# A hybrid decoder layer on one core: nine buffers for gathered index keys, and work moved at the opening and at the output block

## The reference

```
h = rmsnorm(x);  z = h @ w_in            # 2048 x 8848, columns shared among the parts below
retention (8 heads of 128): rotary on q, k; chunks of 128 tokens
    o = (q k^T * decay) v + (q s) * q_decay;  s' = g^c s + (k * k_decay)^T v
    r = head_group_norm(o) * silu(gate)
sparse attention (8 query heads, 2 kv heads), for each query:
    score = sum_h w_h * relu(q_h . k_idx)  over 16 index heads
    top 128 keys (prompt) or top 256 of 4097 cached and new keys (samples)
    a = softmax(q k_sel^T / sqrt(128)) v_sel * silu(gate)
y = rmsnorm(x + concat(r, a) @ w_out)    # 2048 x 2048
```

## Time and profile before

| | |
|---|---|
| median of 3 runs | 1228.62 us |
| the profiled execution | 1228.03 us |
| its span | 1225.6 us |
| TensorE busy | 1173.5 us (96%) |
| VectorE, ScalarE, GpSimd busy | 628.8, 452.2, 569.7 us |
| mean granted TensorE clock | 0.994 |

### The profile page before, as it was taken

How to read it: one execution, slowest core, us unless ns; L and a number is a source line. 1 busy time by engine, 2 the same in 40 slices (tenths; PEclk the granted TensorE clock), 3 DMA queues, 4 the chain that set the end, 5 groups by cost and what they waited for, 6 DMA issues and landing times.

```text
span 1225.6 us, 21932 instructions
## 1 busy us (share of the span) xinstructions
PE 1173.5 (96%) x9168; PEld 1107.1 (90%) x9168; DVE 628.8 (51%) x1198; ACT 452.2 (37%) x790; POOL 569.7 (46%) x255
## 2 busy tenths in 40 slices
PE   6999999888999999999999989999999999999995
PEld 4999996446999999999999989999999998999995
DVE  6600005997996995799997314343442546010013
ACT  5332225664223333333424323442524252233332
POOL 2346454241433333223635485946666384535450
PEclk9999999999999999999999999999999999999998
DMA  7333435272232222222243416445353425432313
GB/s 243 103 108 107 137 103 205 97 258 94 70 115 93 70 70 84 92 70 69 70 124 98 112 35 175 112 114 159 104 152 91 140 70 189 143 103 74 98 35 139
DMA packets 152840, 138.58 MB, mean 113 GB/s; under 512 B 4653, under 2 KB 145053, under 8 KB 151069
## 3 DMA queue, kind: packets, MB, share of 16 engines
q1 hardware_dynamic: 144502, 110.72, 30.1%
q0 software_dynamic: 6976, 22.03, 5.5%
q10 hardware_dynamic: 1280, 4.66, 1.0%
HBM read 127.02 MB, written 10.34 MB: 112 GB/s over the span
## 4 chain that ended last, share of the span: by engine, by line
PE 81%; DVE 10%; DMA 4%; POOL 2%; issue 2%; ACT 1%; another core or an unknown queue 0%; DVEq 0%; ACTq 0%; POOLq 0%
PE bank L1440 23%; PE bank L1441 23%; PE bank L1442 23%; PE bank L1458 4%; DMA kx<-in_cache_kidx,pidx 3%; DVE bm L1077 2%; PE bank L1645 1%; PE bank L1663 1%; DVE cand L1143 1%; DVE top L1139 1%; DVE besti L1141 1%; DMA XT<-in_x_prompt 1%; PE bank L1685 1%; POOL rowf L889 1%; PE bank L1818 1%
## 5 line engine op out<-in xcount | busy, mean ns | idle before, releaser
L1440 PE MATMUL bank<-Hh,Wh 128*128 128x264 f32 (+2 forms) x2432 | 711.2, 292 | 3.0 <-DVE Hl L1277 0.8
L1441 PE MATMUL bank<-Hl,Wh 128*128 128x264 f32 (+2 forms) x2432 | 702.4, 289 | 0.8 <-issue 0.8
L1442 PE MATMUL bank<-Hh,Wl 128*128 128x264 f32 (+2 forms) x2432 | 701.1, 288 | 0.0
L839 POOL TENSOR_TENSOR Wl<-Wraw,Wh 128x2048 fp32r<-128x2048 f32 x84 | 387.2, 4610 | 476.6 <-ACT Wh L487 475.9
L1440 PEld LDWEIGHTS bank<-Hh,Wh 128*128 128x128 f32 x2432 | 458.7, 189 | 8.6 <-issue 4.2
L1441 PEld LDWEIGHTS bank<-Hl,Wh 128*128 128x128 f32 x2432 | 458.5, 189 | 3.0 <-issue 2.7
L1442 PEld LDWEIGHTS bank<-Hh,Wl 128*128 128x128 f32 x2432 | 457.6, 188 | 0.5 <-issue 0.5
L487 ACT ACTIVATE Wh<-Wraw 128x2048 fp32r<-128x2048 f32 x84 | 160.4, 1911 | 362.9 <-PE bank L1442 362.7
L1380 DVE TENSOR_TENSOR Y<-Y,bank 128x512 f32 (+1 forms) x16 | 10.4, 685 | 159.2 <-PE bank L1458 159.2
L1060 DVE COPY QS<-mix 128x128 f32<-128x128 f32 x1 | 0.3, 275 | 140.5 <-ACT mix L493 140.5
L865 POOL DMA_INDIRECT kx<-in_cache_kidx,pidx x32 | 30.3, 947 | 52.6 <-PE bank L1458 46.1
(11 more groups left out here) (255 smaller groups left out, 1230.6 us busy)
## 6 DMA issues: line engine op xcount, KB each, us to landing
Wraw<-in_w_in SPq DMA_DIRECT2D x36, 1024.0 KB
Wraw<-in_w_in SPq DMA_DIRECT2D x64, 512.0 KB
Wraw<-in_w_out SPq DMA_DIRECT2D x16, 1024.0 KB
XT<-in_x_prompt ACTq DMA_DIRECT2D x4, 1024.0 KB, 9.1
sp__96<-in_state_ret SPq DMA_DIRECT2D x8, 512.0 KB, 4.1
out<-sp__96 SPq DMA_DIRECT2D x8, 512.0 KB, 5.3
Y<-in_x_prompt SPq DMA_DIRECT2D x1, 4096.0 KB
out<-Y SPq DMA_DIRECT2D x4, 1024.0 KB
```

The lines of the kernel that those rows point to most:

```text
L839: nc.gpsimd.tensor_tensor(Wl[:, a, :, :], Wraw[:, a, :, :], Wh[:, a, :, :].bitcast(F32), ALU.subtract).then_inc(w_lo, 1)
L1440: mm(bank[i][:, 0:w], wh, Hh[:, kk, s], start=(a == 0 and k == 0), stop=False)
L1441: mm(bank[i][:, 0:w], wh, Hl[:, kk, s], start=False, stop=False)
L1442: last = mm(bank[i][:, 0:w], wl, Hh[:, kk, s], start=False, stop=(a == 1 and k == KC - 1))
```

## The change

It has five parts.

1. Opening: tiles 2 and 3 are turned earlier (tile 2 right behind the samples, tile 3 ahead of `index_weights`), 24 transposes of the constant stand ahead of the first turn (in bank 6), 8 instead of 24 behind the second, and 4 between the key halves go.
2. Cached keys: nine buffers `kx` instead of six; the six slots of `kT` move into `mix`, where gates are stored later. Buffers 2 to 4 lie where `kT` and the new index keys were, so GpSimd waits for `kin_out` before gather 2 and ScalarE doesn't.
3. Retention head 0: 12 top-k steps instead of 14 ahead of `gate(7)`.
4. Output block: `outputs(7)` moves behind the first part of block 35, `turn_outputs(7)` from ahead of the third part to ahead of the fourth; on VectorE three of four `mix_low(1)` go ahead of the samples' norm, the fourth behind `gated(7)`.
5. Tail: GpSimd multiplies the samples' rows by the gain too; the last scaling of y_sample is shared between VectorE and ScalarE.

```diff
+NKX = 9
-        kT, o3 = place("kT", [P, 6, T], F32, o)
-        QS, o3 = place("QS", [P, NS * 32], F32, o3)
+        kT = mix[:, 0:6, 0:T]
+        QS, o3 = place("QS", [P, NS * 32], F32, o + 3 * 4 * KPR * P)
-        for i in range(6):
-            off = (at["scores"][0], at["best"][0])[i] if i < 2 else o3
+        for i in range(NKX):
+            off = (at["scores"][0], at["best"][0])[i] if i < 2 else o + 4 * KPR * P * (i - 2) if i < 5 else o3
...
+            sp.wait_ge(fin_act, 3)
             store(y_sample.rearrange("b o m -> (b o) m"), Ys[:, :])
...
-            act.wait_ge(kin_out, 32)
             for u in range(4):
                 keys_out(u)
...
             y_scale(2)
+            nc.scalar.activation(Ys[:, LASTC // 2:LASTC], Ys[:, LASTC // 2:LASTC], ACT.Copy,
+                                 scale=st4[0:NS, 44:45]).then_inc(fin_act, 1)
...
             for v in range(4 * 8):
                 s, b = v // NS, v % NS
-                if v >= 6:
-                    w = v - 6
+                if v == 2:
+                    pool.wait_ge(kin_out, 32)
+                if v >= NKX:
+                    w = v - NKX
                     pool.wait_ge(kx_tr, 8 * (w // 4) + 4 + w % 4 + 1)
...
                 nc.gpsimd.tensor_tensor(Y[:, :, c], Y[:, :, c], gfb[:, c].unsqueeze(1).to_broadcast([P, QT, 256]),
-                                        ALU.mult).then_inc(y_gain, 1)
+                                        ALU.mult)
+                nc.gpsimd.tensor_tensor(Ys[:, c], Ys[:, c], gfb[0:NS, c], ALU.mult).then_inc(y_gain, 1)
...
-            def mix_low(half):
+            def mix_low(half, which=range(4)):
-                for i in range(KC * half + 1, KC * half + KC, 2):
+                for i in range(KC * half + 1 + 2 * which.start, KC * half + 1 + 2 * which.stop, 2):
...
                 if h == 0:
-                    topk(14)
+                    topk(12)
                     gate(7)
...
             samples_low(KC, 1)
+            mix_low(1, range(3))
             dve.wait_ge(os_ev, NH)
...
             gated(NH - 1)
+            mix_low(1, range(3, 4))
             dve.wait_ge(gs_tr, 1)
...
-            mix_low(1)
             samples_low(0, 2)
...
-            v_.scalar_tensor_tensor(Ys[:, :], Ys[:, :], st4[0:NS, 44:45], gfb[0:NS, :], ALU.mult, ALU.mult).then_inc(fin_dve, 1)
+            v_.scalar_tensor_tensor(Ys[:, LASTC:DM], Ys[:, LASTC:DM], st4[0:NS, 44:45], gfb[0:NS, LASTC:DM], ALU.mult, ALU.mult)
+            v_.tensor_scalar(Ys[:, 0:LASTC // 2], Ys[:, 0:LASTC // 2], st4[0:NS, 44:45], None, ALU.mult).then_inc(fin_dve, 1)
...
-            def chunk(n, a, between=None, step=None, at_=2):
+            def chunk(n, a, between={}, step=None):
-                    if place_ == at_ and between:
-                        between()
+                    if place_ in between:
+                        between[place_]()
...
-            pe.wait_ge(x_norm, 1)
+            keep_busy(24, 6)
             turn_tokens(0)
             turn_tokens(1)
...
-            keep_busy(24)
+            keep_busy(8, 3)
             pe.wait_ge(h_lo, 8)
             pe.wait_ge(w_lo, 1)
             index_keys(0, slice(0, CUT))
             turn_tokens(2)
-            keep_busy(4)
+            turn_tokens(3)
             pe.wait_ge(w_lo, 2)
             index_keys(1, slice(0, CUT)).then_inc(acc_done, 1)
-            turn_tokens(3)
+            turn_tokens(4)
             index_weights(slice(P, CUT))
-            turn_tokens(4)
...
-            outputs(NH - 1)
-            chunk(NB_IN, 0, lambda: turn_outputs(NH - 1))
+            chunk(NB_IN, 0, {1: lambda: outputs(NH - 1), 3: lambda: turn_outputs(NH - 1)})
```

More of the change, by code:

```diff
@@ L161, in build @@
         kx = []
-        for i in range(6):
-            off = (at["scores"][0], at["best"][0])[i] if i < 2 else o3
+        for i in range(NKX):
+            off = (at["scores"][0], at["best"][0])[i] if i < 2 else o + 4 * KPR * P * (i - 2) if i < 5 else o3
             t_, o4 = place(f"kx{i}", [P, KPR * P], F32, off)
             kx.append(t_)
-            o3 = o4 if i >= 2 else o3
+            o3 = o4 if i >= 5 else o3
         assert at["kx1"][0] + 4 * KPR * P <= persist
@@ L238, in build @@
         ws_ready = sem("ws_ready"); ws_zero = sem("ws_zero"); ws_tr = sem("ws_tr"); wsel_ready = sem("wsel_ready"); qs_ready = sem("qs_ready")
-        pidx_ready = sem("pidx_ready"); kx_in = [sem(f"kx_in{i}") for i in range(6)]
+        pidx_ready = sem("pidx_ready"); kx_in = [sem(f"kx_in{i}") for i in range(NKX)]
         kx_tr = sem("kx_tr"); kt_ev = sem("kt_ev"); kq_mm = sem("kq_mm")
@@ L861, in _ @@
                 s, b = v // NS, v % NS
-                if v >= 6:
-                    w = v - 6
+                if v == 2:
+                    pool.wait_ge(kin_out, 32)
+                if v >= NKX:
+                    w = v - NKX
                     pool.wait_ge(kx_tr, 8 * (w // 4) + 4 + w % 4 + 1)
                 nc.gpsimd.indirect_dma_start(
-                    kx[v % 6][:, :], None, cpages,
-                    bass.IndirectOffsetOnAxis(ap=pidx[:, b, s:s + 1], axis=0)).then_inc(kx_in[v % 6], 16)
+                    kx[v % NKX][:, :], None, cpages,
+                    bass.IndirectOffsetOnAxis(ap=pidx[:, b, s:s + 1], axis=0)).then_inc(kx_in[v % NKX], 16)
             lo_loop(10, 19)
@@ L1463, in _, with keep_busy @@
                 mm(bank[i][:, :], ones[:, :], grow[:, 512 * i:512 * i + 512], start=True, stop=True).then_inc(g_mm, 1)
+            def keep_busy(times, b):
+                for _ in range(times):
+                    turn(bank[b][:, 0:P], ident[:, :])
             pe.wait_ge(s_ident, 16)
@@ L1480, in _ @@
             turn(bank[7][:, 0:KT + NH], gn[:, :], KT + NH).then_inc(g_tr, 1)
-            pe.wait_ge(x_norm, 1)
+            keep_busy(24, 6)
             turn_tokens(0)
             turn_tokens(1)
-            def keep_busy(times):
-                for _ in range(times):
-                    turn(bank[3][:, 0:P], ident[:, :])
             def index_keys(a, s):
@@ L1565, in turn_keys @@
                 v, half = 4 * (G // 2) + j, G % 2
-                pe.wait_ge(kx_in[v % 6], 16 * (v // 6 + 1))
+                pe.wait_ge(kx_in[v % NKX], 16 * (v // NKX + 1))
                 if u >= 3:
@@ L1570, in turn_keys @@
                     c = P * (KPR // 2 * half + q)
-                    last = turn(bank[3 + u % 3][:, P * q:P * q + P], kx[v % 6][:, c:c + P])
+                    last = turn(bank[3 + u % 3][:, P * q:P * q + P], kx[v % NKX][:, c:c + P])
                 last.then_inc(kx_tr, 1)
@@ L1619, in _ @@
             last.then_inc(sc_row, 1)
-            chunk(9, 0, lambda: pe.wait_ge(sc_out, 3), at_=1)
+            chunk(9, 0, {1: lambda: pe.wait_ge(sc_out, 3)})
             chunk(9, 1)
@@ L1788, in turn_new_values @@
                     turn(bank[5][0:G3, 0:P], pads[:, 1, :]).then_inc(vs_tr, 1)
-                chunk(n + 1, 1, turn_new_values, at_=3)
+                chunk(n + 1, 1, {3: turn_new_values})
                 pe.wait_ge(acc_free, 4 * (n + 1) + 2)
```

## The result

After takes 1221.01 us (median of 5 runs, 1220.36 to 1221.92), before in the same series 1229.22: ratio 0.9934, 95% interval 0.9923 to 0.9944. That is 8.2 us faster; forecast were 12.4 less, and the time lies 0.5 us above the forecast range (1211.5 to 1220.5). The profiled execution took 1220.82 us (span 1219.0), 7.2 less than that of before.

The account below looks back on a forecast made before the run. It took TensorE, 81% of the chain, to bound the kernel. Opening 3.2, cached keys 6.3, head 0 1.3, output block 1.4 and tail 0.2 sum to 12.4 us off the median 1228.62: 1216.2 us, range 1211.5 to 1220.5.

Parts of the forecast that it names:

- the term for the cached keys: Cached-key stage: nine buffers end the waits for gathers; 6.3 us gained, bounds 4.0 and 8.7.
- The prediction's own signs of being wrong: Cached-key stage: wrong if gathers still end waits, or if the product pitch stays near 4.1 us on average.
- Rival (a): Cached-key stage: ScalarE bounds it, hand-overs 0.4 us worse at each of 14 boundaries, 5 us lost, 1221; chance 0.12.
- untouched: Retention head 2: the longest other wait, before L1818, stays as it is, since TensorE must await GpSimd's rounding anyway.
- Rival (e): Output loop's six turns above all: head 2's stall of late TensorE signals recurs, 5 us each, slower than before; chance 0.04.
- the opening's 3.2: Opening: earlier turns leave VectorE nearly gapless, late index keys start at 39.7; 3.2 us gained, bounds 1.3 to 4.0.
- head 0's 1.3: Retention head 0: two top-k steps less remove the wait at L1822; 1.3 us gained, bounds 0 and 1.3.
- a tail worth nothing: Tail: y_sample's last scaling split over two engines, its store queued with y_prompt's; 0.2 us gained, bounds 0 and 1.2.
- The output block's 1.4: Output block: new waits of 2.1 and 0.8 us against 4.3 before; 1.4 us gained, bounds -1.0 and 3.5.
- rival (c): Output block: samples' low half costs over 3.3 us of waiting, the clock falls, 2 us worse than before, 1219.6; chance 0.08.
- rival (b): Whole kernel: everything pays in full, 3.9 + 8.7 + 1.3 + 3.5 + 0.9 = 18.3 us, time 1210.3; chance 0.10.
- rival (d): Opening: the 24 early turns do not lift the clock, up to 2 us lost of 3.2, time 1218.2; chance 0.06.

Follow-up runs that it names:

- e1: The kernel after with its cached-key part taken back (six buffers, old layout and waits): ratio to before 0.9943.
- e2: The kernel before with the cached-key part alone added: ratio to before 0.9979.
- e4: The kernel after with gathers 7 to 9 held back until 36 of the 48 prompt index scores are added up: ratio to before 0.9927.
- e16: The kernel after with a pause between gathers 5 and 6 of the first nine, until 20 prompt index scores are added up: ratio to before 0.9923.
- e5b: The kernel after with every cached-key gather fetching 512 bytes a row, as many issues at the same points (results not valid): ratio to before 0.9918.
- e7: The kernel after with a pair's four gathers in the key stage issued one every two turned half tiles: ratio to before 0.9911.
- e17: The kernel after with spread and late gathers, eight key slots, a fourth turn bank, and head 2's small gathers in rows of 6, 5 and 5: 1210.25 us, ratio 0.9853.
- e8: The kernel after without the 24 idle turns ahead of the first token tile: ratio to before 0.9925.
- e15: The kernel after with the opening's old order of turns and its four idle turns between the key halves: ratio to before 0.9960.

## Why the prediction was wrong

**What failed** is the term for the cached keys, "8 x 3.4 + 6 x 3.85 = 50.3 ... I take 6.3 us": 2.8 came. Its working did not fail. With the four gathers of a pair spread, the same kernel needs 50.83 us, each interval 3.47 or 3.84, the copy's chain through six slots as it was laid out. What failed is the step behind it, which gives the gathers beside the stage no price ("bandwidth is no limit", "GpSimd's 32 issues stay"): they go three or four in a row at the earliest moment, and ScalarE is held up, mostly until 0.8 to 1.0 us behind the last of them; that costs 3.5 us in all. In before the same rows of four stood beside TensorE's waits for the gathers themselves. The prediction's own signs of being wrong did not catch this: no gather ended a wait, and the average pitch was 3.88, not 4.1. Rival (a), 5 us missing and 1221, met the measured time with the wrong cause: the hand-over costs nothing above its 3.47 (0.07 more than forecast, where it has 0.4), and of the 5.8 missing only 3.5 are in this stage.

**What was missing** is the 1.4 us in the prompt index scores. The forecast has the three further tiles "loaded before the stage, beside prompt index work", at no price. e1, e2, e4 and e16 show the price: a row of nine against rows of six or fewer.

**Head 2** was called "untouched". The stall was; its cover was not, since GpSimd's rounding came sooner: the block behind started 0.5 us later than the rounding allowed and ran at the low clock, at half pace, for 1.1 us more, which makes the 1.0. Rival (e) had the right mechanism (late signals of TensorE) but looked for it in the six turns of the output loop, where it did not come. Where it came, there was a row of gather issues.

**What held**: the opening's 3.2 (by order and fewer idle turns; the raised clock gave 0.1), head 0's 1.3, and a tail worth nothing. The output block's 1.4 held by luck: the new wait of 2.1 came at the place named, but the 0.8 for the samples' norm did not, and the low clock behind the 2.1, worth 1.2 us, was not priced. The prediction prices such a loss only behind a wait of over 3.3 us, in rival (c). That rival (b)'s sum takes 3.9 and 0.9 where the bounds are 4.0 and 1.2 changes nothing. That turns lift the clock is shown by the 16 turns at 1.97 us behind them, and 3.47 without. The Trainium skill (TensorE: Matmul & The Clock Gate, Part 4: PE-mode transpose), behind rival (d), says that a transpose does not count as busy in the same way, and the measurement decides. For the time it made no difference, since VectorE was the later one either way.

**Still open**: how the issuing of gathers holds up the others. In the key stage it takes bytes and issues together (e5b against e7), in the scores mainly the number in a row, in head 2 gathers of one word a row are enough. Late code is not shown to be the way: the stretch of the key stage shown has a 16 KB instruction packet at 248.2 us, amid the gathers' traffic, but e7 has one at 245.3, amid its own, and no delay; most of the long intervals have none, and neither has the stall in the scores.

## What to carry to other kernels

A buffer that comes free sooner lets transfers start sooner and closer together: price the row that they form, not only each one's landing time. If a deeper ring gives less than its waits promised, hold each issue back to where it is still in time; here one changed wait gave as much as the three further buffers. And before a stall is removed, look at who is next: in head 2 each of three splits freed TensorE from one wait and met GpSimd or VectorE within the same head. A wait can also cost what the clock takes behind it: in the output block 1.2 us behind a wait of 2.1.

## What the runs showed of the hardware

- GpSimd's gather issues take 0.94 us and 0.30 between them, whether for 512 KB or 512 bytes. Rows of eight or nine stopped TensorE, VectorE or ScalarE near their end, TensorE for 0.5 to 3.6 us; rows of five or six did so nowhere but for one idle stretch of 0.40 us of TensorE in e17.
- Three or four full gathers in a row (four are 2.1 MB) held ScalarE up, in five places of six until 0.8 to 1.0 us behind the last issue, though TensorE's turn was done before; the same gathers with pauses of 0.9 and 1.9 us between (e7) did not.
- 24 turns of a constant lifted TensorE's clock to 2.4 GHz; a pause of 3.37 us behind 1.97 us of work brought 1.2 GHz back in after (3.50 us for 16 turns), while in e7 the same 16 turns took 2.36. In after a wait of 2.10 us at 1012.5 was followed by 3.4 us at 1.2 GHz (granted clock 0.50), in e8 and e15 the same wait was not.
